# A fourth group of seven block products in the late loop pairs of an FFN input stage, and three low parts made by accumulating DMAs

## The chip, the cores and the metric

The kernel runs on one core of one Trainium2 chip. The metric is the device time of the whole program in microseconds (us), as the median of several executions. Engines are named as the profile names them: PE is TensorE's matmul row and PEld its weight loads, DVE is VectorE, ACT is ScalarE, POOL is GpSimd, and SP is SyncE, which issues the loads.

## What is computed

One encoder layer on 256 tokens of width 2048, all in float32. The change touches the two feed-forward blocks, and in them only the first product (`x @ w_in`, 2048 to 2 x 5632).

```python
def swiglu(x, w_in, w_out):
    gate, up = jnp.split(x @ w_in, 2, axis=-1)
    return (jax.nn.silu(gate) * up) @ w_out

h = h + 0.5 * swiglu(rmsnorm(h, ffn1_norm), ffn1_w_in, ffn1_w_out)
z = rmsnorm(h, mix_norm) @ w_mix_in           # then gMLP and stick-breaking attention
...
h = h + y @ w_mix_out
h = h + memory_cross_attention(...)
h = h + 0.5 * swiglu(rmsnorm(h, ffn2_norm), ffn2_w_in, ffn2_w_out)
return rmsnorm(h, final_norm)
```

## The kernel before

**Products in three parts.** Each float32 operand is split into a high part (rounded to the format that TensorE multiplies fast) and a low part (the rest). A product of two blocks is three matmuls: high by high, high by low, low by high. The helper `three` in `ffn_in` of TensorE's program (L2197 to L2199) writes them. One matmul has 128 rows of tokens and 512 columns of weights.

**Units and the ring.** Weights come in units of 512 KB, two blocks of 128 x 512 (`UK` = 2). SP loads them into `raw`, a ring of four slots (`RING` = 4, L540). For each unit ScalarE copies `raw` to `w_hi` (`split`, L819), and VectorE subtracts to get `w_lo` (L1331). Three counters carry the order: `w_hi_done`, `w_lo_done` and `w_used`. A load of unit u waits until `w_lo_done` has counted unit u - 4. ScalarE's copy of unit u waits for its load and until `w_used` has counted unit u - 4. TensorE waits for `w_lo_done` of the unit and counts `w_used` when it has read it. Every engine runs its own instruction list strictly in order.

**The input stage of an FFN (`ffn_in`).** The 11264 columns are worked in pairs of 512 gate and 512 up columns. The first pair is written out. Pairs j = 1 to 10 are loops of 16 units each (`PAIR` = 16): 1 to 4 are the early ones (`DC` = 4), which also turn a finished block of the hidden activations, and 5 to 10 are the late ones. Each FFN has six late pairs, the kernel twelve.

**Groups of seven products.** In each loop pair, three groups (`FAST` = 3) work on two units together, which hold the four blocks of a 2 x 2 block product, with seven block products where eight would be needed. `weight_sums` on VectorE makes three sums of weight blocks in `t_raw` and one in place in `raw` (L1455, L1456, L1458, L1460; the second of them, L1456, releases ScalarE through `t1_done`). ScalarE then copies the group's two units and the three sums (`t_hi_part`, L916). VectorE makes the low parts of the two units and of the sums (`t_lo_part`, L1472). The matching mixes of the activations (`mix_hi`, `mix_lo`) are made once, in the first pair. TensorE's `fast` does two products on the first unit, then waits for `t_lo_done`, does three products with the sums (p7, p6 and a third; the last counts `t_used`), and then two on the second unit. The other ten units of a pair are plain: four block products each. The order is a list:

```python
for s in range(FAST):
    order += [("fast", s), ("fast", s)] + plain[:2]
    plain = plain[2:]
return order + plain
```

So TensorE does group, two plain units, group, two plain units, group, six plain units.

**Draining a pair.** The seven products leave sums in four PSUM tiles of their own. When the last group has been done, ScalarE copies `sum_p1` (L928), and VectorE adds the sums to the gate columns (L1491, L1494, L1499, L1501, in `pair`). After L1501 (`gate_added`) ScalarE applies silu (L934) and copies the last unit of the pair. VectorE takes the last tile off the up sums (L1506). In the next pair, after the low parts of its first group, VectorE drains the up columns (`up_drained`, L1431), and after the second group it multiplies gate and up (`hidden`, L1438). These are placed by hand between the splits in `pair`.

## Time and profile before

| | |
|---|---|
| median of 3 runs | 2093.14 us (2092.31 to 2094.14) |
| the profiled execution's own time | 2092.97 us |
| its span, first to last instruction | 2091.0 us |
| PE busy | 2082.4 us (100%), 9333 matmuls |
| DVE busy | 1688.7 us (81%) |
| ACT busy | 1144.1 us (55%) |
| POOL busy | 38.3 us (2%) |
| q1, the queue of SP's loads | 464.11 MB, 70.6% of the 16 DMA engines' span |
| q0, the queue of POOL's transfers | 6.82 MB, 1.0% |
| granted TensorE clock, mean | 1.000 |

Busy times of PE overlap a little at their ends, since matmuls are pipelined; start-to-start distances in the timeline are the true pace. The timeline gives each record's start and duration; an engine's next record may start slightly before the recorded end of the one before.

### The profile page before, as it was taken

How to read it: one execution, taken by the hardware profiler on the slowest of the kernel's cores; microseconds unless marked ns; L12 is line 12 of the kernel's file. 1: busy time of each engine (PE TensorE's matmuls, PEld its weight loads, DVE VectorE, ACT ScalarE, POOL GpSimd, SP SyncE). 2: the span in 40 equal slices, each digit the busy share in tenths (PEclk: the TensorE clock that was granted, in tenths of full speed). 3: DMA queues.
4: the chain of work that ended last, by engine and by line, in shares of the span. 5: the costliest groups of instructions: out<-in, count | busy, mean ns of one | idle time of the engine just before them, and what ended most of it. 6: DMA issues, size and time to landing. Idle time of an engine off the chain costs nothing.

```text
span 2091.0 us, 26502 instructions
## 1 busy us (share of the span) xinstructions
PE 2082.4 (100%) x9333; PEld 1730.2 (83%) x9333; DVE 1688.7 (81%) x1897; ACT 1144.1 (55%) x1311; POOL 38.3 (2%) x50
## 2 busy tenths in 40 slices
PE   9999999999999999999999999999999999999998
PEld 8888888888888888888888888888888888888887
DVE  7999999889998676566565656569999899989986
ACT  7555555555555565456544555455555555555554
POOL 0000000000000040000000000000000000000000
PEclk9999999999999999999999999999999999999999
DMA  8777666678777877875588766686767666689664
GB/s 290 227 234 237 214 214 217 218 230 270 228 239 230 276 229 215 249 213 186 173 285 244 234 208 186 186 257 205 231 217 231 229 202 212 219 263 282 199 202 161
DMA packets 185329, 472.51 MB, mean 226 GB/s; under 512 B 17056, under 2 KB 67616, under 8 KB 185120
## 3 DMA queue, kind: packets, MB, share of 16 engines
q1 hardware_dynamic: 183088, 464.11, 70.6%
q0 software_dynamic: 1728, 6.82, 1.0%
q8 instruction: 48, 0.79, 0.1%
q10 hardware_dynamic: 432, 0.53, 0.1%
q14 instruction: 33, 0.27, 0.0%
HBM read 443.60 MB, written 27.79 MB: 225 GB/s over the span
## 4 chain that ended last, share of the span: by engine, by line
PE 99%; issue 0%; ACT 0%; DVE 0%; ACTq 0%; POOLq 0%; DVEq 0%; POOL 0%
PE acc L2174 12%; PE acc L2176 12%; PE acc L2177 12%; PE acc L2197 11%; PE acc L2199 11%; PE acc L2198 11%; PE acc L2267 6%; PE acc L2266 6%; PE acc L2265 6%; PE aux L2197 1%; PE aux L2198 1%; PE aux L2199 1%; PE tp L2199 1%; PE tp L2197 1%; PE tp L2198 1%; PE acc L2391 1%
## 5 line engine op out<-in xcount | busy, mean ns | idle before, releaser
L819 ACT ACTIVATE w_hi<-raw 128x1024 fp32r<-128x1024 f32 x765 | 800.5, 1057 | 749.5 <-PE acc L2177 287.3
L1331 DVE TENSOR_TENSOR w_lo<-raw,w_hi 128x1024 fp32r<-128x1024 f32 x765 | 925.9, 1223 | 298.7 <-ACT w_hi L819 294.8
L2174 PE MATMUL acc<-w_hi,a_hi 128*128 128x512 f32 x616 | 239.9, 389 | 0.0
L2176 PE MATMUL acc<-w_lo,a_hi 128*128 128x512 f32 x616 | 239.7, 389 | 0.0
L2177 PE MATMUL acc<-w_hi,a_lo 128*128 128x512 f32 x616 | 239.7, 389 | 0.0
L2197 PE MATMUL acc<-w_hi,a_hi 128*128 128x512 f32 x460 | 178.9, 389 | 0.0
L2198 PE MATMUL acc<-w_lo,a_hi 128*128 128x512 f32 x460 | 178.9, 389 | 0.0
L2199 PE MATMUL acc<-w_hi,a_lo 128*128 128x512 f32 x460 | 178.9, 389 | 0.0
L2197 PE MATMUL acc<-w_hi,b_hi 128*128 128x512 f32 x460 | 178.9, 389 | 0.0
L2198 PE MATMUL acc<-w_lo,b_hi 128*128 128x512 f32 x460 | 178.9, 389 | 0.0
L2199 PE MATMUL acc<-w_hi,b_lo 128*128 128x512 f32 x460 | 178.9, 389 | 0.0
L2174 PE MATMUL acc<-w_hi,b_hi 128*128 128x512 f32 x448 | 175.5, 392 | 0.0
L2176 PE MATMUL acc<-w_lo,b_hi 128*128 128x512 f32 x448 | 174.4, 389 | 0.0
L2177 PE MATMUL acc<-w_hi,b_lo 128*128 128x512 f32 x448 | 174.4, 389 | 0.0
L2265 PE MATMUL acc<-w_hi,hid_hi 128*128 128x512 f32 x432 | 168.0, 389 | 0.0
L2266 PE MATMUL acc<-w_lo,hid_hi 128*128 128x512 f32 x432 | 168.0, 389 | 0.0
L2267 PE MATMUL acc<-w_hi,hid_lo 128*128 128x512 f32 x432 | 168.0, 389 | 0.0
L2177 PEld LDWEIGHTS acc<-w_hi,a_lo 128*128 128x128 f32 x616 | 115.6, 188 | 24.2
L2174 PEld LDWEIGHTS acc<-w_hi,a_hi 128*128 128x128 f32 x616 | 115.7, 188 | 23.9
L2176 PEld LDWEIGHTS acc<-w_lo,a_hi 128*128 128x128 f32 x616 | 115.7, 188 | 23.6
L1472 DVE TENSOR_TENSOR t_lo_part<-t_raw,t_hi_part 128x1536 fp32r<-128x1536 f32 x60 | 105.5, 1758 | 1.6 <-ACT t_hi_part L916 1.1
L2199 PEld LDWEIGHTS acc<-w_hi,a_lo 128*128 128x128 f32 x460 | 86.4, 188 | 18.1
(358 smaller groups left out, 3217.3 us busy)
## 6 DMA issues: line engine op xcount, KB each, us to landing
raw<-in_ffn_w_in SPq DMA_DIRECT2D x349, 512.0 KB, 4.2
raw<-in_ffn_w_out SPq DMA_DIRECT2D x176, 512.0 KB, 4.3
raw<-in_w_mix_in SPq DMA_DIRECT2D x80, 512.0 KB, 4.3
raw<-in_w_ckv SPq DMA_DIRECT2D x64, 512.0 KB, 4.3
memq<-bounce SPq DMA_DIRECT2D x196, 128.0 KB, 4.4
bounce<-stage SPq DMA_DIRECT2D x35, 512.0 KB, 5.1
raw<-in_w_mix_out SPq DMA_DIRECT2D x32, 512.0 KB, 4.3
raw<-in_w_cq SPq DMA_DIRECT2D x32, 512.0 KB, 4.3
```

The source lines that it names most:

```text
L819: eng.activation(w_hi[:, u % RING], raw[:, u % RING], ACT.Copy).then_inc(w_hi_done, 1)
L1331: eng.tensor_tensor(w_lo[:, u % RING], raw[:, u % RING], w_hi[:, u % RING].bitcast(f32), ALU.subtract).then_inc(w_lo_done, 1)
L1472: eng.tensor_tensor(t_lo_part[:], t_raw[:], t_hi_part[:].bitcast(f32), ALU.subtract).then_inc(t_lo_done, 1)
L2174: eng.matmul(dst, x_hi[:, rows], w_hi[:, slot, i], start=start and i == 0, stop=False)
L2176: eng.matmul(dst, x_hi[:, rows], w_lo[:, slot, i], start=False, stop=False)
L2177: last = eng.matmul(dst, x_lo[:, rows], w_hi[:, slot, i], start=False, stop=stop and i == UK - 1)
L2197: eng.matmul(dst, x[0], w[0], start=start, stop=False)
L2198: eng.matmul(dst, x[0], w[1], start=False, stop=False)
L2199: return eng.matmul(dst, x[1], w[0], start=False, stop=stop)
L2265: eng.matmul(dst, x[0], w[0], start=start, stop=False)
L2266: eng.matmul(dst, x[0], w[1], start=False, stop=False)
L2267: return eng.matmul(dst, x[1], w[0], start=False, stop=stop)
```

## The change

In the late pairs the order of units is a new list, with four groups instead of three (`MIXES` = 4) and eight plain units instead of ten. Ahead of each of the first three groups stands one plain unit (at positions 0, 3 and 6, `LATE_ADDED_AT`). It is loaded and copied at that position, but TensorE takes it after the group's two units (`LATE_TAKEN`). Its high and low parts are not in the ring but in tiles of their own (`added`). ScalarE makes the high part and, with a second activation of scale -1, minus the high part in the low tile. GpSimd then issues a DMA that adds the unit's weights from HBM onto that tile (`accum_op=ALU.add`). TensorE waits for the DMA's semaphore (`lo_added`). VectorE makes no low part for these three units; it counts `w_lo_done` for them with the first of the four sums of the following group, which therefore waits until ScalarE has made both copies. TensorE's order is: group 0, unit 0, group 1, unit 3, group 2, unit 6, group 3, and five plain units. The activations' mixes for the fourth group are made in the first pair (a fourth entry in `X_MIX_AT` and `H3_MIX_AT`). The late pairs drain in a new `late_pair`, in which VectorE makes one more unit's low part before L1491's addition, and another one before L1501's.

```diff
+MIXES = 4
+ADDED = 3
+def late_order():
+    plain = [(side, u) for side in range(2) for u in range(MIXES, U8)]
+    order, taken = [], []
+    for s in range(MIXES):
+        at = len(order) + (s < ADDED)
+        taken += [at, at + 1]
+        if s < ADDED:
+            taken.append(len(order))
+            order.append(plain.pop(0))
+        order += [("fast", s), ("fast", s)]
+    return order + plain, taken + list(range(len(order), PAIR))
...
-X_MIX_AT = [5, 7, 9]
-H3_MIX_AT = [9, 11, 13]
+X_MIX_AT = [5, 7, 9, 12]
+H3_MIX_AT = [7, 9, 11, 13]
...
+            def lo_parts_added(w, base):                          # GpSimd
+                for j in range(DC + 1, FJ):
+                    for x, p in enumerate(LATE_ADDED_AT):
+                        eng.wait_ge(w_hi_done, base + PAIR * j + p + 1)
+                        eng.dma_start(added[x][1][:].rearrange("p k n -> p (k n)"), w[PAIR * j + p],
+                                      accum_op=ALU.add).then_inc(lo_added[x], 16)
...
+                def added_hi(j, x):                               # ScalarE
+                    ...
+                    eng.wait_ge(w_loaded[p % RING], 16 * loads + 16)
+                    eng.wait_ge(w_used, base + PAIR * j - PAIR + LATE_END)
+                    eng.activation(added[x][0][:], raw[:, p % RING], ACT.Copy)
+                    eng.activation(added[x][1][:], raw[:, p % RING], ACT.Copy, scale=-1.0).then_inc(w_hi_done, 1)
+                def late_pair(j):
+                    for s in range(MIXES):
+                        if s < ADDED:
+                            added_hi(j, s)
+                        fast_hi(j, s, LATE_FAST_AT[s], late_count(base, j, s))
+                    for p in range(LATE_END, PAIR - 3):
+                        split(base, j, p, PAIR)
+                    eng.wait_ge(w_used, base + PAIR * j + LATE_END)
+                    eng.activation(copy_p1, sum_p1, ACT.Copy).then_inc(p1_copied, 1)
+                    split(base, j, PAIR - 3, PAIR)
+                    split(base, j, PAIR - 2, PAIR)
+                    eng.wait_ge(gate_added, fast_pairs[base] + j)
+                    ...                                           # silu of both halves
+                    split(base, j, PAIR - 1, PAIR)
...
+                    if unit_added is not None:                    # VectorE, weight_sums
+                        eng.wait_ge(w_hi_done, unit_added + 1)
+                        eng.tensor_tensor(t_raw[:, 0], b12, b22, ALU.add).then_inc(w_lo_done, 1)
...
+                def late_pair(j):                                 # VectorE
+                    done = fast_pairs[base] + j
+                    for s in range(MIXES):
+                        p, count = LATE_FAST_AT[s], late_count(base, j, s) + 1
+                        weight_sums(j, s, p, count, ...)
+                        fast_lo(j, p, count)
+                        if s == 0:
+                            up_drained(j - 1)
+                        if s == 1:
+                            hidden(j - 1, 0)
+                            hidden(j - 1, 1)
+                    for p in range(LATE_END, PAIR - 2):
+                        unit_lo(j, p)
+                    eng.wait_ge(p1_copied, done)
+                    eng.tensor_tensor(shared[:, 0], sum_p6, copy_p1, ALU.add).then_inc(p6_added, 1)
+                    eng.wait_ge(w_used, base + PAIR * j + LATE_GATE_END)
+                    eng.wait_ge(sent, 16 * number(TURNS, hid) + 16 * j)
+                    eng.tensor_tensor(stage[:, 0], acc[:, 0], copy_p1, ALU.add)
+                    eng.wait_ge(p6_added, done)
+                    eng.tensor_tensor(shared[:, 1], shared[:, 0], sum_p7, ALU.subtract).then_inc(p7_added, 1)
+                    unit_lo(j, PAIR - 2)
+                    eng.wait_ge(p7_added, done)
+                    eng.tensor_tensor(stage[:, 1], acc[:, 1], shared[:, 1], ALU.add).then_inc(gate_added, 1)
+                    eng.wait_ge(gate_added, done)
+                    p5 = sum_p5.rearrange("p (a n) -> p a n", a=1).broadcast_to([P, NT, CH])
+                    eng.tensor_tensor(shared[:], shared[:], p5, ALU.subtract).then_inc(gate_read, 1)
+                    unit_lo(j, PAIR - 1)
...
+                    x = LATE_ADDED_AT.index(p) if groups == MIXES and p in LATE_ADDED_AT else None   # TensorE, plain
+                    if x is not None:
+                        eng.wait_ge(lo_added[x], 16 * added_count(base, j))
+                    else:
+                        eng.wait_ge(w_lo_done, base + PAIR * j + p + 1)
...
+                with eng.Fori(DC + 1, FJ) as j:
+                    eng.wait_ge(gate_read, silus[base] + j)
+                    for p in LATE_TAKEN:
+                        if p in LATE_FAST_AT:
+                            s = LATE_FAST_AT.index(p)
+                            fast(j, s, p, late_count(base, j, s), MIXES)
+                        elif LATE_ORDER[p][0] != "fast":
+                            plain(j, p, LATE_ORDER, MIXES)
```

## Rows read from the trace of the kernel before

**Rows 1.** Waits of TensorE, whole run: who waited for whom, us in total, times, longest.

```profile
PE aux L2382 <- POOL ones L711: 1.1, 1, 1.1
PE acc L2391 <- ACT w_hi L1026: 0.6, 1, 0.6
```

**Rows 2.** Busy time by engine in the late pair j = 6: us, busy (instructions), clock, DMA, GB/s.

```profile
258.82:300.31 41.49, 41.49 (x185) 34.37 (x184) 37.73 (x40) 22.52 (x22) 0.00 (x0) 1.00 0.68 215
```

**Rows 3.** Timeline of TensorE: first matmuls of pairs 6 and 7 (start, duration).

```profile
258.82 0.39 PE L2197 MATMUL tp<-w_hi,a_hi 128*128 128x512 f32 x1
...
300.30 0.39 PE L2197 MATMUL tp<-w_hi,a_hi 128*128 128x512 f32 x1
```

**Rows 4.** Timeline of VectorE in pair 6, around its second group.

```profile
259.01 1.23 DVE L1431 TENSOR_TENSOR shared<-acc,shared 128x1024 f32<-128x1024 f32 x1
...
261.31 0.68 DVE L1455 TENSOR_TENSOR t_raw<-raw 128x512 f32<-128x512 f32 x1
...
263.89 2.36 DVE L1331 TENSOR_TENSOR w_lo<-raw,w_hi 128x1024 fp32r<-128x1024 f32 x2
266.25 1.76 DVE L1472 TENSOR_TENSOR t_lo_part<-t_raw,t_hi_part 128x1536 fp32r<-128x1536 f32 x1
...
271.45 1.41 DVE L1438 SCALAR_TENSOR_TENSOR stage<-shared,rstd,stage 128x512 f32<-128x512 f32 x2
```

**Rows 5.** Timeline of VectorE, end of pair 6 and first group of pair 7.

```profile
284.80 0.69 DVE L1491 TENSOR_TENSOR shared<-aux,arrived 128x512 f32<-128x512 f32 x1 [1.71 <-ACT arrived L928]
...
288.10 0.68 DVE L1501 TENSOR_TENSOR stage<-acc,shared 128x512 f32<-128x512 f32 x1
...
291.13 1.23 DVE L1331 TENSOR_TENSOR w_lo<-raw,w_hi 128x1024 fp32r<-128x1024 f32 x1
292.27 0.68 DVE L1455 TENSOR_TENSOR t_raw<-raw 128x512 f32<-128x512 f32 x1
...
297.53 1.76 DVE L1472 TENSOR_TENSOR t_lo_part<-t_raw,t_hi_part 128x1536 fp32r<-128x1536 f32 x1 [0.15 <-ACT t_hi_part L916]
```

**Rows 6.** Timeline of ScalarE over the same stretch.

```profile
284.18 0.60 ACT L928 ACTIVATE arrived<-tp 128x512 f32<-128x512 f32 x1 [2.34 <-PE acc L2199]
284.67 1.05 ACT L819 ACTIVATE w_hi<-raw 128x1024 fp32r<-128x1024 f32 x1
...
288.81 1.34 ACT L934 ACTIVATE stage<-stage,rstd 128x512 f32<-128x512 f32 x2 [0.85 <-DVE stage L1501]
290.06 1.04 ACT L819 ACTIVATE w_hi<-raw 128x1024 fp32r<-128x1024 f32 x1
...
295.06 1.06 ACT L819 ACTIVATE w_hi<-raw 128x1024 fp32r<-128x1024 f32 x1 [0.23 <-PE acc L2199]
296.02 1.48 ACT L916 ACTIVATE t_hi_part<-t_raw 128x1536 fp32r<-128x1536 f32 x1
```

**Rows 7.** Timeline of ScalarE, the turned block at the end of pair 4.

```profile
209.35 1.06 ACT L826 ACTIVATE b_hi<-out_t_raw 128x1024 f32 x1 [0.62 <-DVE out_t_raw L1371]
```

**Rows 8.** DMA issues, whole run: transfer, issuer, count, KB each, median us to landing.

```profile
raw<-in_ffn_w_in SPq DMA_DIRECT2D x349, 512.0 KB, 4.2
...
row_gain<-in_final_norm POOLq DMA_DIRECT2D x1, 1024.0 KB, 9.9
row_gain<-in_ln_v_gain POOLq DMA_DIRECT2D x1, 512.0 KB, 5.5
...
ws_t<-in_ws_cols POOLq DMA_DIRECT2D x1, 512.0 KB, 15.7
```

**Rows 9.** DMA issues from 669 to 680 us (two POOL transfers).

```profile
raw<-in_ffn_w_out SPq DMA_DIRECT2D x4, 512.0 KB, 4.7
```

**Rows 10.** DMA issues from 717 to 735 us (six POOL transfers).

```profile
raw<-in_w_mix_in SPq DMA_DIRECT2D x6, 512.0 KB, 7.0
```

**Rows 11.** Timeline of TensorE, the first products of the run.

```profile
6.41 1.05 PE L2391 MATMUL acc<-w_hi,a_lo 128*128 128x512 f32 x2
...
10.46 0.63 PE L2391 MATMUL acc<-w_hi,a_hi 128*128 128x512 f32 x2
```

More of the change, by code:

```diff
@@ L396, in encoder_block @@
         w_used = sem("w_used")
+        lo_added = [sem(f"lo_added{x}") for x in range(ADDED)]
         t_full = sem("t_full")
@@ L937, in pair @@
                     split(base, j, PAIR - 1, PAIR)
-                    if hid_dst is not None:
-                        fill_hi(turned, number(TURNS, hid) + j, hid_dst, src=turned_hid)
+                    fill_hi(turned, number(TURNS, hid) + j, hid_dst, src=turned_hid)
+                def added_hi(j, x):
+                    p = LATE_ADDED_AT[x]
+                    loads = slot_loads(base, p % RING) + p // RING + rate(p, PAIR) * j
+                    eng.wait_ge(w_loaded[p % RING], 16 * loads + 16)
[14 more added lines that the diff above has]
+                    eng.wait_ge(gate_added, fast_pairs[base] + j)
+                    for t in range(NT):
+                        last = eng.activation(stage[:, t], stage[:, t], ACT.Silu,
+                                              scale=rstd[:, stat(rs), t:t + 1])
+                    last.then_inc(silu_done, 1)
+                    split(base, j, PAIR - 1, PAIR)
                 first(silu)
@@ L2220, in fast @@
                     three(sum_p5, s1, ring_block(p, 0), start, stop).then_inc(w_used, 1)
-                    eng.wait_ge(t_lo_done, fast_count(base, j, s) + 1)
+                    eng.wait_ge(t_lo_done, count + 1)
                     three(sum_p7, s3, sum_block(0), start, stop)
```

133 lines of the change are left out of this document (84 added, 49 removed).

## The prediction, made before the change was run

> **What bounds the kernel now.** I read the waits of TensorE first. Over the whole run there are two, 1.1 and 0.6 us, both at the start [rows 1]: wherever the change acts, the time is the number of matmuls times their pace. The table of busy times for one late pair says how near the others are: in 41.49 us VectorE is busy 37.73, ScalarE 22.52, and the granted clock is 1.00 [rows 2]. The timeline gives the pace. A late pair has 3 groups x 21 + 10 plain units x 12 = 183 matmuls, and the first matmuls of pairs 6 and 7 are 41.48 us apart [rows 3], so one matmul is 0.2267 us, a plain unit (12) 2.72, a group (21) 4.76, and the six matmuls of a group ahead of its wait for `t_lo_done` 1.36. TensorE issues without a gap. VectorE has 3.8 us to spare in a pair, but that is an average; what matters is how early each group's `t_lo_part` is ready, so I laid out the order of VectorE's and ScalarE's work around it.
>
> **What the change takes away.** A late pair becomes 4 x 21 + 8 x 12 = 180 matmuls: 3 fewer, 0.68 us. Twelve late pairs: 36 matmuls, 8.2 us. That is all it can gain.
>
> **VectorE's sum.** It loses three units, 3 x 1.14 = 3.4 us (291.13 to 292.27 [rows 5]), and gains a fourth set of sums, 2.58 (261.31 to 263.89), and a fourth `t_lo_part`, 1.76 recorded and about 1.68 to the next start [rows 4], as each record's end overlaps the next by 0.08. Net +0.8, so some 38.6 of 40.8 us. By busy shares it fits. By order it does not, as follows. Times are relative to a named event; 0.03 to 0.2 is the release seen in the rows.
>
> **Step 1, the wait at the first group of a pair.** Call F the end of the pair's last group on TensorE. Now F of pair 6 is 258.82 + 111 x 0.2267 = 283.98, six plain units (16.3 us) follow, and the next group needs its `t_lo_part` at F + 17.7. It ends at 297.53 + 1.76 = 299.29, F + 15.3 [rows 5]: 2.4 us early. After the change five plain units follow: it is needed at F + 5 x 2.72 + 1.36 = F + 14.96. The chain to it:
> ScalarE's `copy_p1` starts at F + 0.20, the copy of the next unit 0.49 later and takes 1.05 [rows 6], so F + 1.74. VectorE now makes that unit's low part first (to F + 2.91), then three additions at 0.60 each (to 4.71), then another unit (to 5.85), then L1501, 0.68 (to F + 6.53). In the kernel before L1501 ends at 288.78, F + 4.8 [rows 5]. Silu starts 0.03 later, and the last unit's copy 1.25 after it (288.81 to 290.06 [rows 6]): F + 7.81. Then come the two new copies of unit 0 of the next pair. Back to back a copy takes 0.96 (295.06 to 296.02): they start at F + 8.8 and 9.7 and end at F + 10.8. Only then may VectorE start the sums (it waits for `w_hi_done` of that unit), where before they started at 292.27, F + 8.3 [rows 5]. From sums to the end of `t_lo_part`: ScalarE's copies start 1.5 after them (two sums, 1.29, and a release), two copies 1.93, `t_hi_part` 1.48, then `t_lo_part` 1.76: 6.7 us. End at F + 17.5, needed at F + 14.96: TensorE waits 2.57 us. The same 6.7 applied before gives 299.0, against 299.29 in the row, where 0.23 was a wait for TensorE.
> This happens between late pairs, 5 times in each FFN: 10 x 2.57 = 25.7 us. Pair 5 follows an early pair: there ScalarE is held by the turned block at 209.35 [rows 7], with the two copies ending at 212.3; 6.7 later is 219.05, needed at 258.82 - 41.48 + 1.36 = 218.70, 0.35 us, twice 0.7. After pair 10 the output stage begins with plain units, where nothing waits for sums: no cost.
>
> **Step 2, the waits at the second and third group.** Between two groups there is now one plain unit, so TensorE returns after 33 matmuls, 7.48 us, instead of 45, 10.2 us. VectorE has sums, two units and `t_lo_part` for each: 2.58 + 2.36 + 1.68 = 6.62 [rows 4]. For group 1 add `up_drained`, 1.15: 7.77. For group 2 add `hidden`, 1.33: 7.95. For group 3 nothing. So TensorE waits 0.29 and 0.47 us, and not at group 3 (0.86 early, which doesn't come back, since F counts from TensorE). 12 x 0.76 = 9.1 us. Before, the 10.2 us hid all of it.
> The loads may add. The second unit of group 1 can be loaded only when the low part of the ring slot's last unit is made; from there to the sums VectorE has 1.18 + 1.68 + 1.15 = 4.0 us, for group 2 1.18 + 1.68 + 1.33 = 4.2. A load lands after 4.2 us in the median [rows 8], after 4.7 beside two POOL transfers [rows 9], after 7.0 beside six [rows 10]. I take 4.7 for group 1, whose load runs wholly beside the first accumulating DMA, and the middle of 4.2 and 4.7 for group 2: +0.7 and +0.25, 12 x 0.95 = 11.4 us. Bounds: +0.2 (2.4 us in all) at 4.2; +5.8 (70 us) at 7.0.
>
> **Step 3, the accumulating DMA.** No row has one. For unit 0 it can start at F + 10.8, and TensorE wants the unit after its group, at F + 17.5 + 3.4 = F + 20.9: 10.1 us, and a further 1.0 in which TensorE would wait at group 1 in any case. For units 3 and 6 the same count gives about 11.5. A POOL transfer of this size landed after 5.5 us, one of twice the bytes after 9.9, the slowest, queued behind five, after 15.7 [rows 8]. I take at most 9.9, since the engines move the unit and read the tile: hidden, nothing added. If it is 15.7, 4.6 us show in each pair, 55 us. Lower bound nothing. The Trainium skill (Collectives: The Full Stack, The bandwidth ceiling) says that an add in a DMA costs not by the adding but by its second source read, so twice a copy's reading; the row of twice the bytes is the same estimate. It also warns (SBUF — State Buffer, Who interferes with whom) that GpSimd's descriptors starve behind VectorE operations of the two-port modes, which subtractions of two tensors are not; the 5.5 us stood beside such work.
>
> **Step 4, the rest.** The fourth mix in the first pair is four small steps and a low part on VectorE, none over 512 columns, so by 0.6 us for 512 (a quarter of 2.58, rounded down) at most 3.0 us. That pair's 16 units take TensorE 43.5 us and VectorE 16 x 1.14 = 18.2; hidden, and at most 2 x 3.0 = 6 us if not. GpSimd's issues have no one behind them in these stages. ScalarE: three copies more and a fourth `t_hi_part`, 4.4 us on 22.5 of 41; only its place in step 1 counts.
>
> **Sum.** -8.2 + 25.7 + 0.7 + 9.1 + 11.4 = +38.7 on the profiled execution's own 2092.97 us, which is 0.2 below the median: **2131.7 us**, 1.8% slower. With loads at 4.2 it is 2093 + 29.7 = 2122.7; at 7.0, 2190.
>
> **Rivals.** A. TensorE stays the bound, and the 36 matmuls are gained: 2093 - 8.2 = 2084.8 us. For it: VectorE's 38.6 busy us fit into 40.8. Against it: it decides only if `t_lo_part` is ready at F + 14.96, and the chain would have to be 2.6 us shorter than rows add up to; nothing I see makes it so. 9%.
> B. The accumulating DMA or the loads beside it are late: 15.7 us to landing gives 2131.7 + 55 = 2187; loads at 7.0 give 2190. For it: three more units from HBM in a pair of 16, and reads of the tile. Against it: even beside two POOL transfers a load took 4.7. 17%.
> C. TensorE's clock falls in the waits. At the start of the run, after idling, ten matmuls of the same shape took 10.46 - 6.41 = 4.05 us, 0.405 each [rows 11], near the pace of 1.2 GHz, against 0.2267 at 2.4 GHz. If each wait of 2.57 us cost such a start-up, about 12 x 0.2 = 2.4 us, that is 10 x 2.4 = 24: 2156 us. Against it: the granted clock is 1.00 throughout, and in a wait of under 3 us in 45 TensorE is nearly always busy. 8%. This is the rule of the Trainium skill (TensorE: Matmul & The Clock Gate, Part 1: The HAM clock gate) that idleness halves the clock.
> D. The waits come but are small, and the gain pays for most of them: within 0.2%, 4%; up to 2108, 2%.
> The forecast, waits of step 1 and 2 with the DMA hidden, 2110 to 2150: 60%.
>
> **Numbers.** About 0.2% (4.2 us) is what a measurement here can tell from no change. Faster is A, 9%; same 4%; slower 60 + 17 + 8 + 2 = 87%. The range 2108 to 2185 leaves out A and D (15%) and the worst of B.
>
> **What would show it.** Each step in the changed trace: 180 matmuls at 0.2267 in a late pair; TensorE idle before its products with the sums, released by `t_lo_part`, 2.6 us once between late pairs and 0.3 to 1.2 at the second and third group, none at the fourth; the pair at 44 to 46 us instead of 41.5; the two ScalarE copies right behind the last unit's, and VectorE's first sum released by them; no wait of TensorE for a DMA. Wrong would be: TensorE waiting for the accumulating DMA (B), or matmuls slower than 0.23 behind a wait (C), or no waits (A). My weakest terms are the loads' 11.4 us and the DMA's 9.9.

## The result, and the profile after

| | before | after |
|---|---|---|
| median of the runs compared | 2093.16 us (2091.77 to 2094.14, 6 runs) | 2158.93 us (2156.15 to 2162.15, 6 runs) |
| the profiled execution's own time | 2092.97 us | 2162.01 us |
| its span | 2091.0 us | 2160.3 us |
| matmuls | 9333 | 9297 |
| granted TensorE clock, mean | 1.000 | 0.999 |

The ratio is 1.0316, with a 95% interval of 1.0303 to 1.0330: 65.8 us slower, where I forecast 38.7 slower. All figures from the trace of after are from its profiled execution, which took 69.0 us more than that of before.

The waits of TensorE, whole run (us in total, times, longest). Before had two waits, of 1.1 and 0.6 us [rows 1]:

```profile
PE aux L2332 <- DVE t_lo_part L1573: 31.8, 39, 1.2
PE tp L2332 <- DVE w_lo L1423: 22.2, 21, 1.7
PE acc L2416 <- DVE w_lo L1423: 1.4, 2, 0.7
```

Two kinds of wait make up nearly all of it, both at the groups: for the low part of the sums (`aux<-t_lo_part`), as forecast, and for the low part of the group's own first unit (`tp`), which VectorE makes in the same run of work. No wait of TensorE is put down to an accumulating DMA (`lo_added`).

The busy time by engine in pair 6, first product to first product, which answers to [rows 2]:

```profile
261.52:308.83 47.31, 42.39 (x181) 33.39 (x181) 38.18 (x42) 26.07 (x27) 2.57 (x3) 1.00 0.75 221
```

The pair takes 47.31 us instead of 41.49. Its 180 matmuls at the pace of before are 40.8 us, so 6.5 us of it are lost at waits. VectorE is busy 38.18 us (I had summed 38.6), with 9 us free in the pair: it is not full, it is late at particular places. The clock is 1.00.

TensorE in pair 7, the first product of each wait (start, duration, idle time before it in brackets; this answers to [rows 3]):

```profile
308.83 0.50 PE L2332 MATMUL tp<-w_hi,a_hi 128*128 128x512 f32 x1 [0.83 <-DVE w_lo L1423]
...
311.66 0.49 PE L2332 MATMUL aux<-t_hi_part,mix_hi 128*128 128x512 f32 x1 [1.17 <-DVE t_lo_part L1573]
...
319.20 0.50 PE L2332 MATMUL tp<-w_hi,a_hi 128*128 128x512 f32 x1 [1.11 <-DVE w_lo L1423]
...
322.06 0.50 PE L2332 MATMUL aux<-t_hi_part,mix_hi 128*128 128x512 f32 x1 [1.20 <-DVE t_lo_part L1573]
...
330.12 0.50 PE L2332 MATMUL aux<-t_hi_part,mix_hi 128*128 128x512 f32 x1 [0.25 <-DVE t_lo_part L1573]
```

The true cost of a wait is the distance between starts, less matmuls times the pace. From 322.06 to 330.12 are 33 matmuls, 7.48 us at the pace, in 8.06 us. Of the 0.58 us between the two, 0.11 stands right behind the product at 322.06 and belongs to the wait before it (that product's duration is 0.50 in place of 0.39), 0.40 stands ahead of the product at 330.12, and the rest is spread. The product at 330.12 is again 0.11 longer, so I counted its wait as 0.40 + 0.11 = 0.51 us, where the bracket says 0.25. Every distance over the pace was counted in this way. By place, over the twelve late pairs:

| place | measured | forecast |
|---|---|---|
| group 0, between late pairs (10) | 25.3 us: 1.10 ahead of the group, 1.43 ahead of its sums | 25.7 |
| group 0, pair 5 (2) | 1.0 | 0.7 |
| group 1 (12) | 33.9 | 3.5 (VectorE) + 8.4 (load) |
| group 2 (12) | 6.1, 0.51 each | 5.6 (VectorE) + 3.0 (load) |
| group 3 (12) | 2.2 | 0 |
| second FFN, first groups of its first two loop pairs | 2.4 | 0 |
| first FFN, first group of its first loop pair | 1.5 | 0 |
| output stages | 2.5 | 0 |
| together | 74.9 | 46.9 |
| 36 matmuls fewer | -8.2 | -8.2 |

That is +66.7 of the 69.0; another 1.2 us stands ahead of a product of the attention stages at 994.42. Most of the miss, 22 us, stands in one row, group 1. VectorE in that stretch, end of pair 6 and the first three groups of pair 7; it answers to [rows 4] and [rows 5]:

```profile
300.09 0.68 DVE L1603 TENSOR_TENSOR stage<-acc,shared 128x512 f32<-128x512 f32 x1
...
303.12 1.23 DVE L1423 TENSOR_TENSOR w_lo<-raw,w_hi 128x1024 fp32r<-128x1024 f32 x1 [1.10 <-ACT w_hi L877]
305.02 0.69 DVE L1552 TENSOR_TENSOR t_raw<-raw 128x512 f32<-128x512 f32 x1 [0.67 <-ACT added_lo L1010]
...
309.84 1.76 DVE L1573 TENSOR_TENSOR t_lo_part<-t_raw,t_hi_part 128x1536 fp32r<-128x1536 f32 x1
311.52 1.22 DVE L1527 TENSOR_TENSOR shared<-acc,shared 128x1024 f32<-128x1024 f32 x1
315.33 0.69 DVE L1552 TENSOR_TENSOR t_raw<-raw 128x512 f32<-128x512 f32 x1 [2.60 <-DMA raw<-in_ffn_w_in]
...
320.24 1.76 DVE L1573 TENSOR_TENSOR t_lo_part<-t_raw,t_hi_part 128x1536 fp32r<-128x1536 f32 x1
...
328.31 1.76 DVE L1573 TENSOR_TENSOR t_lo_part<-t_raw,t_hi_part 128x1536 fp32r<-128x1536 f32 x1
...
331.23 0.69 DVE L1554 TENSOR_TENSOR t_raw<-raw 128x512 f32<-128x512 f32 x1 [1.17 <-DMA raw<-in_ffn_w_in]
```

Read from the top. At 305.02 the sums of group 0 start, released by ScalarE's second copy of the added unit: step 1's chain, link by link. At 315.33 the sums of group 1 start 2.60 us late, and what they wait for is a load. ScalarE over the first part of it, which answers to [rows 6]:

```profile
300.80 1.34 ACT L1028 ACTIVATE stage<-stage,rstd 128x512 f32<-128x512 f32 x2 [3.87 <-DVE stage L1603]
302.05 1.04 ACT L877 ACTIVATE w_hi<-raw 128x1024 fp32r<-128x1024 f32 x1
302.99 1.04 ACT L1009 ACTIVATE added_hi<-raw 128x1024 fp32r<-128x1024 f32 x1
303.94 1.04 ACT L1010 ACTIVATE added_lo<-raw 128x1024 fp32r<-128x1024 f32 x1
```

And the DMA issues between 305 and 312 us, the stretch ahead of that late load (median us from issue to landing last; the plain loads answer to [rows 9]):

```profile
raw<-in_ffn_w_in SPq DMA_DIRECT2D x3, 512.0 KB, 6.3
added_lo<-in_ffn_w_in POOLq DMA_DIRECT2D x2, 512.0 KB, 7.9
```

Over the whole run the same two kinds are:

```profile
raw<-in_ffn_w_in SPq DMA_DIRECT2D x349, 512.0 KB, 4.4
...
added_lo<-in_ffn_w_in POOLq DMA_DIRECT2D x36, 512.0 KB, 7.5
```

The whole-run median of the loads hardly moved (4.2 before [rows 8], 4.4 after). In this stretch, beside an accumulating DMA, it is 6.3, though of three loads only. By the landings in the trace, 83 loads of the late pairs stood more than half their time beside an accumulating DMA and took 5.7 us in the median; 67 stood beside none and took 4.1. The median over 349 loads hides the few that matter.

### The profile page after: what moved, and what is told of

Read it like the earlier page. It is cut to its first block, busy times and chain, and to the rows that moved or that the text cites. A ratio compares the mean times of both kernels' runs of the same rounds, so it can differ in the third digit from the quotient of the medians.

```text
span 2160.3 us, 26666 instructions
## 1 busy us (share of the span) xinstructions
PE 2094.5 (97%) x9297; PEld 1715.3 (79%) x9297; DVE 1697.3 (79%) x1931; ACT 1185.0 (55%) x1361; POOL 69.3 (3%) x86
## 4 chain that ended last, share of the span: by engine, by line
PE 67%; DVE 13%; DMA 8%; issue 6%; ACT 5%; SPq 1%; ACTq 0%; DVEq 0%; POOL 0%; POOLq 0%
PE acc L2311 9%; PE acc L2309 9%; PE acc L2312 9%; DMA raw<-in_ffn_w_in 6%; PE acc L2416 5%; PE acc L2417 5%; PE acc L2418 5%; DVE w_lo L1423 5%; PE acc L2334 4%; PE acc L2333 4%; PE acc L2332 4%; ACT w_hi L877 3%; DVE t_lo_part L1573 2%; PE aux L2332 1%; PE aux L2333 1%
## 5 line engine op out<-in xcount | busy, mean ns | idle before, releaser
L877 ACT ACTIVATE w_hi<-raw 128x1024 fp32r<-128x1024 f32 x729 | 756.0, 1055 | 703.8 <-PE acc L2312 274.4
L1423 DVE TENSOR_TENSOR w_lo<-raw,w_hi 128x1024 fp32r<-128x1024 f32 x729 | 878.6, 1222 | 324.1 <-ACT w_hi L877 323.4
L2309 PE MATMUL acc<-w_hi,a_hi 128*128 128x512 f32 x616 | 239.9, 389 | 0.0
L2311 PE MATMUL acc<-w_lo,a_hi 128*128 128x512 f32 x616 | 239.7, 389 | 0.0
L2312 PE MATMUL acc<-w_hi,a_lo 128*128 128x512 f32 x616 | 239.7, 389 | 0.0
L2309 PE MATMUL acc<-w_hi,b_hi 128*128 128x512 f32 x448 | 175.6, 392 | 0.0
L2312 PE MATMUL acc<-w_hi,b_lo 128*128 128x512 f32 x448 | 174.4, 389 | 0.0
L2311 PE MATMUL acc<-w_lo,b_hi 128*128 128x512 f32 x448 | 174.4, 389 | 0.0
L2312 PEld LDWEIGHTS acc<-w_hi,a_lo 128*128 128x128 f32 x616 | 115.6, 188 | 24.2
L2332 PE MATMUL acc<-w_hi,a_hi 128*128 128x512 f32 x346 | 134.7, 389 | 0.0
L2332 PE MATMUL acc<-w_hi,b_hi 128*128 128x512 f32 x346 | 134.7, 389 | 0.0
L2333 PE MATMUL acc<-w_lo,a_hi 128*128 128x512 f32 x346 | 134.6, 389 | 0.0
L2333 PE MATMUL acc<-w_lo,b_hi 128*128 128x512 f32 x346 | 134.6, 389 | 0.0
L2334 PE MATMUL acc<-w_hi,a_lo 128*128 128x512 f32 x346 | 134.6, 389 | 0.0
L2334 PE MATMUL acc<-w_hi,b_lo 128*128 128x512 f32 x346 | 134.6, 389 | 0.0
L977 ACT ACTIVATE t_hi_part<-t_raw 128x1536 fp32r<-128x1536 f32 x72 | 106.1, 1473 | 0.0
```

Of the source, the lines that this page charges most:

```text
L877: eng.activation(w_hi[:, u % RING], raw[:, u % RING], ACT.Copy).then_inc(w_hi_done, 1)
L1423: eng.tensor_tensor(w_lo[:, u % RING], raw[:, u % RING], w_hi[:, u % RING].bitcast(f32), ALU.subtract).then_inc(w_lo_done, 1)
L2309: eng.matmul(dst, x_hi[:, rows], w_hi[:, slot, i], start=start and i == 0, stop=False)
L2311: eng.matmul(dst, x_hi[:, rows], w_lo[:, slot, i], start=False, stop=False)
L2312: last = eng.matmul(dst, x_lo[:, rows], w_hi[:, slot, i], start=False, stop=stop and i == UK - 1)
L2332: eng.matmul(dst, x[0], w[0], start=start, stop=False)
```

## The experiments

Twelve kernels, each beside runs of the kernel before. Medians in us, lowest and highest in brackets:

| kernel | what it is | time | ratio to before, 95% interval |
|---|---|---|---|
| after | the change | 2158.9 (2156.2 to 2162.2) | 1.0316 (1.0303 to 1.0330) |
| e1_no_dma | no accumulating DMAs | 2136.7 (2135.8 to 2138.5) | 1.0210 (1.0193 to 1.0227) |
| e2_copy_dma | plain copies in their place | 2145.6 (2142.4 to 2147.2) | 1.0246 (1.0229 to 1.0263) |
| e3_vector_lo | VectorE makes the three low parts | 2160.7 (2158.6 to 2161.9) | 1.0322 (1.0304 to 1.0339) |
| e4_drain_order | VectorE's drain order of before | 2139.2 (2137.8 to 2142.4) | 1.0223 (1.0206 to 1.0240) |
| e5_copies_early | e4, first added unit copied before silu | 2153.6 (2146.3 to 2159.7) | 1.0298 (1.0280 to 1.0316) |
| e6_spread | e5, drains spread over four groups | 2137.0 (2136.3 to 2139.6) | 1.0211 (1.0194 to 1.0228) |
| e7_three_groups | the DMAs alone, three groups | 2130.2 (2129.0 to 2130.7) | 1.0178 (1.0161 to 1.0194) |
| e8_early_no_dma | e5 without DMAs | 2119.4 (2119.3 to 2121.4) | 1.0125 (1.0108 to 1.0142) |
| e9_spread_no_dma | e6 without DMAs | 2123.2 (2122.4 to 2127.0) | 1.0150 (1.0133 to 1.0167) |
| e10_three_no_dma | e7 without DMAs | 2113.8 (2112.3 to 2114.5) | 1.0099 (1.0082 to 1.0116) |
| e11_product_first | e10, one product of TensorE moved | 2098.1 (2096.5 to 2099.9) | 1.0025 (1.0015 to 1.0035) |
| e12_slack | e6 with more slack for the sums | 2137.0 (2135.8 to 2139.6) | 1.0213 (1.0196 to 1.0230) |

### What the accumulating DMAs cost: e1, e2, e3

```diff
-            lo_parts_added(ffn1_w_in, FFN1_IN)
...
-            lo_parts_added(ffn2_w_in, FFN2_IN)
...
-                        eng.wait_ge(lo_added[x], 16 * added_count(base, j))
+                        eng.wait_ge(w_hi_done, base + PAIR * j + p + 1)
```

> The changed kernel without its 36 accumulating DMAs; TensorE takes a plain unit's own tiles as soon as ScalarE has made them (the low parts then lack the weights, so the output is not the reference's). My theory: the second group's loads are late because they run beside such a DMA. Then the waits at group 1 (33.9 us in twelve pairs) fall to about 8, those at group 0 (26.3 us) stay: 2133 us. Rival, order alone: the load of the second group is late by its place in the ring, and nothing changes: 2159 us. Rival, the DMAs cause all waits: 2090 us.

Measured 2136.7: without the DMAs 22.2 us are gone, though TensorE never waited for one. The waits of TensorE and of VectorE's sums:

```profile
PE aux L2330 <- DVE t_lo_part L1571: 23.9, 38, 1.2
PE tp L2330 <- DVE w_lo L1421: 9.2, 12, 0.8
```

```profile
DVE t_raw L1550 <- DMA raw<-in_ffn_w_in: 5.2, 8, 1.0
```

The sums waited 43.3 us for loads in after (31.0 at L1552 and 12.3 at L1554) and wait 5.2 here. Group 0 keeps its 1.10 and 1.44 us; group 1 falls to 0.5 to 1.4, and what group 3 lost is gone. The loads' share of the loss is the DMAs' doing.

Next, the same transfers and issues, but plain copies, without the read of the tile:

```diff
                         eng.dma_start(added[x][1][:].rearrange("p k n -> p (k n)"), w[PAIR * j + p],
-                                      accum_op=ALU.add).then_inc(lo_added[x], 16)
+                                      ).then_inc(lo_added[x], 16)
```

> The changed kernel with the same 36 DMAs as plain copies from HBM instead of additions (the low parts are then the weights themselves, the output is not the reference's). If what slows the loads beside it is the second read that an addition needs, the waits at group 1 fall by about half, to 2145 us; if it is the first 512 KB alone, 2158 us, as with the addition.

Measured 2145.6. The copies landed after 4.7 us in the median instead of 7.5, and they cost 8.9 us of the 22.2; the adding costs the other 13.4. That each accumulating transfer weighs more than a copy is shown; that the weight lies in the second read is the likely reading, and the Trainium skill (Collectives: The Full Stack, The bandwidth ceiling) puts the cost there too: not the add but its second source read is paid, about twice a copy's. The 7.5 us against 4.7 here, 1.6 times, go the same way and not as far.

```diff
-                    eng.activation(added[x][0][:], raw[:, p % RING], ACT.Copy)
-                    eng.activation(added[x][1][:], raw[:, p % RING], ACT.Copy, scale=-1.0).then_inc(w_hi_done, 1)
+                    eng.activation(added[x][0][:], raw[:, p % RING], ACT.Copy).then_inc(w_hi_done, 1)
...
+                        eng.tensor_tensor(added[x][1][:], raw[:, slot], added[x][0][:].bitcast(f32),
+                                          ALU.subtract).then_inc(w_lo_done, 1)          # VectorE
```

> The fourth group alone: the three units keep their own tiles and their place, but VectorE makes their low parts (1.14 us each, ahead of the group's sums), ScalarE makes one copy instead of two, and there is no DMA. My theory: no late loads (2133 us as without DMAs), but VectorE's order is the bound: + 1.14 at groups 1 and 2 and + 0.2 at group 0, 12 x 2.5 = 30 us: 2163 us. Rival, VectorE's sum decides: 42 us of work in a pair against 40.8 of TensorE, 1.2 us a pair: 2100 us.

Measured 2160.7, beside 2158.9 with the DMAs. The DMAs do take 3.4 us per pair off VectorE and three copies' time is added to ScalarE, but what they give there they take back through the loads: the two ways of making the low parts cost the same here. The waits stand elsewhere, though: in e3 VectorE's sums wait for no load, groups 1 and 2 lose about 1.5 us each and group 0 about 2.9.

### The chain at the first group: e4, e5

e4 gives VectorE the order of the drains of before, with one unit's low part fewer ahead of L1501's addition:

```diff
-                    for p in range(LATE_END, PAIR - 2):
+                    for p in range(LATE_END, PAIR - 3):
                         unit_lo(j, p)
...
                     eng.tensor_tensor(shared[:, 0], sum_p6, copy_p1, ALU.add).then_inc(p6_added, 1)
+                    unit_lo(j, PAIR - 3)
...
-                    unit_lo(j, PAIR - 2)
                     eng.tensor_tensor(stage[:, 1], acc[:, 1], shared[:, 1], ALU.add).then_inc(gate_added, 1)
+                    unit_lo(j, PAIR - 2)
```

> The changed kernel with the late pairs drained in the order of the kernel before (first addition ahead of the low part of the third last unit, silu's addition ahead of that of the second last). My theory: silu, and with it the next pair's first sums, come 1.74 us earlier, and the wait at group 0 shrinks from 2.5 to 0.8 us at ten places: 17 us less, 2142 us. Rival: the wait at group 0 comes from the two copies for the added unit or from the load, and stays: 2159 us.

Measured 2139.2, 19.8 us under after. The wait ahead of group 0 went from 1.10 to 0 to 0.2 us, the one ahead of its sums stayed at 1.35 to 1.45. Start to start, in the two profiled executions (23.4 us apart), that is some 10 us less at group 0 and some 13 us less at group 1, which I had not expected. TensorE's waits for `w_lo`, which stood at both groups, fell from 22.2 to 1.8 us in all. So the drain's new order makes 1.1 us of the late start of a pair. The other 1.4 us have a second cause right behind it, as VectorE's first sum of pair 7 shows:

```profile
305.47 0.69 DVE L1552 TENSOR_TENSOR t_raw<-raw 128x512 f32<-128x512 f32 x1 [1.35 <-DMA raw<-in_ffn_w_in]
```

In after this sum was released by ScalarE's second copy of the added unit; here the copy ends at 304.77 and a load comes 0.7 us later.

e5 adds to e4 that ScalarE copies the next pair's first added unit ahead of silu, under a counter of its own:

```diff
                     split(base, j, PAIR - 2, PAIR)
+                    if more:
+                        added_hi(j + 1, 0)
                     eng.wait_ge(gate_added, fast_pairs[base] + j)
```

> The changed kernel with the drain order of before and, beside it, ScalarE's two copies of each pair's first added unit made ahead of the silu of the pair before, where ScalarE idles, with a semaphore of their own. My theory: the next pair's sums then start at F + 8.3 as in the kernel before, t_lo_part is ready at F + 15.0 where it is needed at F + 14.96, and the wait at group 0 is nearly gone: 15 us less than with the drain order alone, and a few more since the first DMA is over before the second group's load: 2120 us. Rival: the wait at group 0 moves to the load of the group's units: 2135 us.

Measured 2153.6, where I expected 2120: a miss, and by direction the rival's (2135), but worse than that too. The copies are early, and so is the accumulating DMA that they release: it now runs beside the loads of group 0's own units. VectorE at that place:

```profile
303.92 1.23 DVE L1432 TENSOR_TENSOR w_lo<-raw,w_hi 128x1024 fp32r<-128x1024 f32 x1 [0.92 <-ACT w_hi L881]
306.52 0.69 DVE L1564 TENSOR_TENSOR t_raw<-raw 128x512 f32<-128x512 f32 x1 [1.37 <-DMA raw<-in_ffn_w_in]
```

The first sum waits for a load, as it already did in e4: the copies that e5 makes earlier were no longer what came last there. Group 1 falls to 0.5 to 0.8 us between late pairs, group 0 rises to between 1.0 and 3.5 us and another 1.5. The disturbance moved with the DMA.

This is also the kernel whose runs differ most, 13 us, and the only one in whose trace the granted clock fell before the end of the run. It fell twice in the second FFN, right behind long waits of TensorE:

```profile
1767.42 0.50 PE L2345 MATMUL tp<-w_hi,b_hi 128*128 128x512 f32 x1 [2.77 <-DVE w_lo L1432]
...
1770.88 0.63 PE L2346 MATMUL aux<-t_lo_part,mix_hi 128*128 128x512 f32 x1
...
1815.76 0.50 PE L2345 MATMUL tp<-w_hi,b_hi 128*128 128x512 f32 x1 [2.31 <-DVE w_lo L1432]
```

From 1770 to 1775 us the granted clock is 0.50 and a matmul starts every 0.43 us in place of 0.23. The two stretches at 1.2 GHz last 6.8 and 3.4 us, which is some 5 us of loss. A wait of 3.19 us at 265.0 in the same run left the clock at 1.00, so the length of one wait alone does not say whether it falls. The mean clock was 0.997 in the runs of 2146.3 and 2151.6 us and 0.993 in those of 2155.6 and 2159.7, against 0.999 in e4. From these means the two slower runs lost, by my estimate, some 12 us to the clock and the two faster ones some 5, which is about half of the 13 us between the runs.

### The drains spread, and no DMAs: e6, e8, e9

e6 cuts `up_drained` and `hidden` into halves, one behind each of the four groups:

```diff
-                        if s == 0:
-                            up_drained(j - 1)
-                        if s == 1:
-                            hidden(j - 1, 0)
-                            hidden(j - 1, 1)
+                        if s < 2:
+                            up_drained_half(j - 1, s)
+                        else:
+                            hidden(j - 1, s - 2)
```

> The same, with VectorE's up_drained and hidden cut in halves, one half behind each of the four groups (the store of the product then issued three units later). If VectorE's work between groups sets the waits at groups 1 and 2, they shrink by 0.3 and 0.5 us, 12 x 0.8: 2110 us. Rival, the load of the group's second unit sets them (4.2 us and more after the low part that frees its slot): they stay, 2119 us.

Measured 2137.0, 16.5 us under e5, but far over my 2110 and the rival's 2119. The sums still wait 29.4 us for loads (27.1 ahead of the first sum, 2.3 ahead of the second).

e8 is e5, and e9 is e6, with the edit of e1 (for the first added unit the wait is on e5's own counter).

> The version with early copies and the drain order of before, without its DMAs (low parts lack the weights, so the output is not the reference's): what a free DMA would give. Without DMAs the changed kernel took 2136.7 us; ten waits of 2.5 us at group 0 go, 25 us, and those at groups 1 and 2 stay: 2112 us. If it comes near 2087 us, the waits at groups 1 and 2 came from group 0's.

Measured 2119.4: the DMAs cost e5 34.2 us, its fallen clock included. What is left between late pairs is 1.4 to 1.8 us at group 0, where the sums wait for the load of the group's second unit, and 0.51 to 0.7 us at each of the next two.

> The spread drains and early copies of e6_spread, with its accumulating DMAs left out (the low parts of three units of a late pair then lack the weights, so the output is not the layer's). Question: how near four groups can come to the gain of 8.2 us when both known costs are taken away. My theory: what is left is the load of the group's own units, 1.5 us at group 0, since SP can issue it only when the low part that frees its slot is made, and 0.5 us of VectorE at one of the other groups; 12 x 2.0 = 24 us on 2084.8, so 2109 us, about 28 us under e6_spread (2137.0). Rival 1: the spreading does nothing when the DMAs are gone (e8_early_no_dma took 2119.4), then 2119. Rival 2: with loads undisturbed and drains spread, nothing waits, and the four groups pay: 2085 to 2090, faster than before.

Measured 2123.2. The first rival held: without the DMAs the spreading gives nothing (it is 3.8 us worse than e8). Groups 1 and 2 still lose 0.51 us each in most pairs, although VectorE has half a drain less there. That constant was the first sign that VectorE's order is not what makes it.

### Three groups: e7, e10, e11

e7 has three groups as before, in the new order and with the DMAs:

```diff
-MIXES = 4
+MIXES = 3
-X_MIX_AT = [5, 7, 9, 12]
-H3_MIX_AT = [7, 9, 11, 13]
+X_MIX_AT = [5, 7, 9]
+H3_MIX_AT = [9, 11, 13]
```

> The accumulating DMAs alone: the changed kernel with three groups in the late pairs, each still behind an added unit, so ten plain units of which three get their low part by DMA and the last seven stand together; 183 matmuls a pair. VectorE has 3.4 us less to do in a pair than in the kernel before. My theory: spacing of one plain unit between groups and late loads make waits of some 3.5 us a pair at groups 1 and 2 whatever VectorE's sum is; none at group 0 (seven plain units ahead of it): 12 x 3.5 = 42: 2135 us. Rival, the fourth group is what makes VectorE late, and with less work for it nothing waits: 2093 us.

Measured 2130.2, against the 2135 of my theory and the 2093 of the rival. e10 is e7 with the edit of e1.

> The order of e7_three_groups (three groups, each with a plain unit ahead of it that is copied into tiles of its own, 183 matmuls), with the accumulating DMAs left out (the low parts of three units of a late pair lack the weights, so the output is not the layer's). VectorE has three low parts less to make than in the kernel before and TensorE the same matmuls. Question: does the new order alone cost time, with no added work and no added transfer? My theory: yes, about half of e7_three_groups's 37 us is the order (one plain unit between two groups in place of two, so the loads and sums of the next group have 7.5 us in place of 10.2) and half the DMAs' traffic: 2110 us. Rival 1: all of it is the traffic: 2093. Rival 2: all of it is the order: 2130.

Measured 2113.8. e10 has TensorE's work of the kernel before, less work for VectorE, three more copies in a pair for ScalarE and no added transfer, yet it takes 21.0 us more. TensorE at the three groups of pair 6 in e10, which all wait alike:

```profile
262.05 0.50 PE L2330 MATMUL aux<-t_hi_part,mix_hi 128*128 128x512 f32 x1 [0.24 <-DVE t_lo_part L1571]
...
270.08 0.50 PE L2330 MATMUL aux<-t_hi_part,mix_hi 128*128 128x512 f32 x1 [0.24 <-DVE t_lo_part L1571]
...
278.12 0.50 PE L2330 MATMUL aux<-t_hi_part,mix_hi 128*128 128x512 f32 x1 [0.24 <-DVE t_lo_part L1571]
```

ScalarE and VectorE between the first and the second of them:

```profile
264.53 1.06 ACT L875 ACTIVATE w_hi<-raw 128x1024 fp32r<-128x1024 f32 x1 [2.43 <-DVE raw L1553]
265.80 1.06 ACT L875 ACTIVATE w_hi<-raw 128x1024 fp32r<-128x1024 f32 x1 [0.21 <-PE acc L2332]
266.76 1.47 ACT L975 ACTIVATE t_hi_part<-t_raw 128x1536 fp32r<-128x1536 f32 x1
```

```profile
265.62 2.50 DVE L1421 TENSOR_TENSOR w_lo<-raw,w_hi 128x1024 fp32r<-128x1024 f32 x2
268.27 1.76 DVE L1571 TENSOR_TENSOR t_lo_part<-t_raw,t_hi_part 128x1536 fp32r<-128x1536 f32 x1
```

The group's second copy, at 265.80, is released by TensorE, which has just finished the previous group. From there: copy 0.96, `t_hi_part` 1.5, `t_lo_part` 1.76, and TensorE goes on at 270.08, 4.3 us later, 4.5 from the end of its group. It has one plain unit and six matmuls to do in that time, 18 x 0.2267 = 4.08 us; the 0.4 that is missing and the 0.11 of a slower first matmul are the 0.51. It is a closed loop of TensorE, ScalarE and VectorE with a period of 8.03 us for 33 matmuls of 7.48 us (0.51 and 0.04 that are spread), whatever VectorE does in the free part of it. In all of e10 it costs 36 x 0.51 = 18.4 of the 21.0 us. By the code the cause is the added unit. With it, 18 matmuls lie between the unit that this copy waits for and the next wait for sums, where 30 did before (6.8 us). At the second and third group the copy would not even have to wait so long: the added unit takes no slot in the ring of `w_hi`, so the slot is free after the previous group's first unit, but the count asks for its end.

e11 changes one thing in it: three matmuls that need no sums come ahead of the wait for them, 21 in place of 18.

```diff
+                    eng.wait_ge(w_lo_done, unit + 2)
+                    three(acc[:, 0], block_of(UK * s + 1, 0), ring_block(p + 1, 0), start, False)
+
                     eng.wait_ge(t_lo_done, count + 1)
                     three(sum_p7, s3, sum_block(0), start, stop)
                     three(sum_p6, s2, sum_block(1), start, stop)
                     three(acc[:, 1], block_of(UK * s + 1, 1), sum_block(2), start, False).then_inc(t_used, 1)
-                    eng.wait_ge(w_lo_done, unit + 2)
-                    three(acc[:, 0], block_of(UK * s + 1, 0), ring_block(p + 1, 0), start, False)
```

> e10_three_no_dma (2113.8 us; three groups, a unit ahead of each, no accumulating DMAs, the low parts of three units lack the weights, so the output is not the layer's) with one change in TensorE's program: in a group, the three matmuls of the second unit's first product come before the wait for the sums and not behind them. In the trace of e10_three_no_dma each of the 36 groups loses 0.51 us before its sums, with the same period of 8.03 us, whatever VectorE has to do between. Theory: this is a closed loop. ScalarE's copy of the group's second unit waits until TensorE has finished the unit four positions before; from TensorE's release to the end of t_lo_part it takes 0.3 + 1.0 + 1.5 + 1.8 = 4.6 us, while TensorE has only 12 + 6 = 18 matmuls, 4.08 us, before it wants the sums. With 21 matmuls, 4.76 us, the loop is no longer too long and all 36 waits go: 18.4 us, 2095 us. Rival: the 0.51 us is VectorE's own order (8.0 us of work between two t_lo_parts against 7.48 us of matmuls); then moving the want by 0.68 us once per group doesn't help the pace between groups of a pair, and only the first group of a pair gains: some 2107 us.

Measured 2098.1, 15.8 us under e10. TensorE at the second group, without a wait, and ScalarE's two copies back to back, no longer released by TensorE:

```profile
266.46 0.39 PE L2332 MATMUL acc<-w_hi,a_lo 128*128 128x512 f32 x1
266.68 0.46 PE L2330 MATMUL aux<-t_hi_part,mix_hi 128*128 128x512 f32 x1
```

```profile
261.41 2.01 ACT L875 ACTIVATE w_hi<-raw 128x1024 fp32r<-128x1024 f32 x2 [2.43 <-DVE raw L1553]
```

The rival (VectorE's own pace, 2107) is out. What VectorE's order does cost, by my reading, is seen now that the loop is gone: 0.07 and 0.31 us at the second and third group of a pair, 4.6 us in twelve.

### More slack, with everything else real: e12

e12 is e6 with that product moved (in the second and third group both products of the second unit), and with counts that let ScalarE copy as soon as the ring slot is truly free:

```diff
+                    if late:
+                        eng.wait_ge(w_lo_done, unit + 2)
+                        three(acc[:, 0], block_of(UK * s + 1, 0), ring_block(p + 1, 0), start, False)
+                    if late and 0 < s < MIXES - 1:
+                        three(acc[:, NT], s4, ring_block(p + 1, 1), start, False).then_inc(w_used, 1)
...
-                    eng.wait_ge(w_used, base + length * n + (u - RING + 1))
+                    eng.wait_ge(w_used, base + length * n + (u - RING + 1 if freed is None else freed))
```

> e6_spread (2137.0 us; four groups, real accumulating DMAs, drains spread, the whole computation) with two changes: in the late pairs TensorE does the second unit's first product (in the second and third group both its products) before it waits for the sums, and ScalarE's copies wait for the unit that really held the ring slot (a unit made in tiles of its own never held one), not for the count four positions back. Theory: in each late pair 0.68 us goes at the first group, up to 1.36 at the second and third, whose waits were 0.5 to 1.05 and 1.0 to 1.6 us; the wait for the first unit's own low part at the first group stays. 12 x (0.7 + 0.8 + 1.2) = 32 us: 2105 us. Lower bound, if the loads then come undisturbed: 2090. Rival: the transfers set the pace, the loads come later by as much as TensorE comes earlier, and less than 10 us are won: 2127 or more. Below 2093 it would be the version that pays.

Measured 2137.0, the same as e6: the rival. VectorE's sums and the loads they wait for:

```profile
DVE t_raw L1584 <- DMA raw<-in_ffn_w_in: 27.1, 25, 2.5
```

and at the second and third group of pair 6:

```profile
267.77 0.69 DVE L1584 TENSOR_TENSOR t_raw<-raw 128x512 f32<-128x512 f32 x1 [0.40 <-DMA raw<-in_ffn_w_in]
...
276.94 0.69 DVE L1584 TENSOR_TENSOR t_raw<-raw 128x512 f32<-128x512 f32 x1 [1.89 <-DMA raw<-in_ffn_w_in]
```

The first sums wait 27.1 us for loads in 25 waits, as in e6. When TensorE and ScalarE come earlier, TensorE loses as much start to start, mostly now ahead of the first unit's low part (15.4 us in 24 waits). With the DMAs in, that leaves the time from a freed slot to a landed load as what binds four groups; no kernel here changed that time alone. No kernel with four groups came below 2119.4 us, and none of the twelve beat the kernel before.

## Why the prediction was right or wrong

**The sign and the account.** Three differences between kernels add up to the loss. The order alone, a unit ahead of each of three groups: e10 less before, 21.0 us. The fourth group on top, without DMAs: e1 less e10, 22.9 us, which is 8.2 gained and 31 lost in waits. The DMAs: after less e1, 22.2 us. Together 66.1, against 65.8 measured. The DMAs' share depends on what else is tight: 16.4 us with three groups (e7 less e10), 13.8 with the drains spread (e6 less e9), 34.2 with the early copies alone (e5 less e8; some of it is e5's fallen clock, some 5 us in its trace).

**What the change takes away.** 36 matmuls fewer and 8.2 us: right, and in no kernel did it pay for one pair's waits.

**Step 1, 25.7 us.** Right, link by link. With F at 294.24 (TensorE's last group of pair 6 ends there), L1603, the addition that was L1501, ends at 300.77, F + 6.53 as forecast; the last unit's copy starts at F + 7.81 as forecast; the added unit's copies end at F + 10.7 (10.8), and `t_lo_part` at F + 17.4 (17.5). 25.3 us measured, where these ten places had 25.7. Without the DMAs (e1) it stays; with the drain order of before (e4) the 1.10 us ahead of the group go and the rest stays, held by a load. So the chain was right, but taking it away could give back only 1.1 of its 2.5 us: the load behind it sets the other 1.4. I placed all of it ahead of the sums, while 1.10 of it falls ahead of the group, at the low part of its first unit.

**Step 2, VectorE's order, 9.1 us.** The sizes looked right (0.47 forecast and 0.51 measured at group 2), the mechanism was not. e10 has the 0.51 at all 36 groups, with a drain behind them or not, and e11 removes it by moving three matmuls. I had checked what ScalarE's copies wait for by the sums (`t1_done`) and never by `w_used`, the count that TensorE gives. What is left to VectorE's own order in e11 is 4.6 us. That I came near the number at group 2 is luck.

**Step 2, the loads, 11.4 us.** This is the step that failed, in size: "I take 4.7 for group 1, whose load runs wholly beside the first accumulating DMA". It took 6.3 us. The formula around it held: sums late by 6.3 less the 4.0 us of VectorE's work is 2.3, and the row shows 2.60; with the 0.29 of VectorE that is 2.9 us, and from 311.66 to 322.06 TensorE loses 2.9. Twelve of these make 33.9 us, where I had 11.9 for the group. I had taken the price of a load beside plain transfers by POOL [rows 9] for one beside transfers that also read their target; the other row, 7.0 beside six transfers [rows 10], was the nearer one.

**Step 3, the accumulating DMA hidden.** Right: landed after 7.5 us in the median and 9.3 at most, against a budget of 10.1, and TensorE never waited for it. But "hidden" was judged by who waits for the transfer itself. Its cost was in its neighbours, 22.2 us.

**Step 4, the rest.** Mostly hidden, not wholly: 2.4 us behind the first pair of the second FFN and 1.5 behind that of the first. In the second FFN the first of the four mixes was moved to an earlier position (`H3_MIX_AT` begins at 7), and ScalarE stands for 3.51 us:

```profile
1446.99 0.31 ACT L952 ACTIVATE b_hi<-stage 128x128 fp32r<-128x128 f32 x1 [3.51 <-PE acc L2312]
```

The loss of about 2 us at that place is in every kernel with four groups and in none with three (e7, e10, e11), so the fourth mix or its place makes it. That it is the move was argued from this row, not tried, and the first FFN, where no mix was moved, lost something too. The 2.2 us at group 3 go with the loads (the 1.17 us wait at 331.23 above; in e1 they are gone); the 2.5 us of the output stages I have not explained.

**The rivals.** A (36 matmuls gained) is out, and e8 shows by how much: even with free DMAs and early copies four groups take 26 us more than before. B was half right: its mechanism, loads late beside the DMAs, added what the forecast lacked, at 6.3 us and not at 7.0. C (a falling clock) is out for the change itself: the mean granted clock stayed at 0.999 of 2.4 GHz, and behind a wait only the first matmul is longer, 0.50 us in place of 0.39, then the pace is 0.23. But its mechanism is real at waits not much longer: in e5 the clock fell to 1.2 GHz behind waits of 2.77 and 2.31 us. The Trainium skill (TensorE: Matmul & The Clock Gate, Part 1: The HAM clock gate) says that idleness halves the clock; in after waits of up to 1.7 us did not bring that about, in e5 the trace agrees.

## What to carry to other kernels

A transfer that nobody waits for is not free: price it by the loads that run beside it and by how few microseconds lie between a freed slot and the need for its load, not by the median of all loads. When work is moved to shorten one engine's list, follow every counter around the ring, the one that TensorE gives back too, and compare the time around each closed loop with the matmuls it has to fit under; here 4.5 us against 4.08 cost 0.5 us at every group, and three matmuls ahead of the wait removed it. Two waits in a row hide each other: an edit of the same kind that gave 15.8 us without the DMAs (e11) gave none with them (e12), and once the drain was in order (e4) a load stood where the copies had.

## What the runs showed of the hardware that was not expected

- An accumulating DMA of 512 KB from HBM into an SBUF tile landed after 7.5 us in the median (5.4 to 9.3, 36 of them); a plain copy of the same size from the same queue after 4.7. Loads of 512 KB beside the accumulating ones took 6.3 us between 305 and 312 us (three loads), against 4.1 in the same stretch of e1_no_dma (two); over all late pairs 5.7 (83 loads), against 4.0 in e1_no_dma (176).
- A blocked TensorE loses more than the idle time that the view of waits shows. In e10_three_no_dma the view lists 9.5 us in 36 waits, 0.26 each, and the start-to-start distances lose 0.51 each, 18.4 us. On top of 0.24 listed come 0.16, by which a record overlaps the next (0.39 long at a pace of 0.2267), and 0.11, by which the first matmul is longer.
- TensorE's clock can fall in the middle of a kernel that is busy 98% of its span. In e5_copies_early it went to 1.2 GHz for 6.8 and 3.4 us behind waits of 2.77 and 2.31 us, while a wait of 3.19 us elsewhere in the same run left it at 2.4 GHz, and its runs differ with the mean clock: 2146 to 2152 us at 0.997, 2156 to 2160 us at 0.993.
